# The stage behind a chunked recurrence, before and after it is cut into four quarters over all engines

## The reference, cut to what matters

```python
S_t = S_{t-1} (diag(w_t) + a_t b_t^T) + v_t k_t^T ;  y_t = S_t r_t      # y_l sums both directions

def rwkv_output(y, r, k, v, g, r_k, lnx_g, lnx_b):
    mu = jnp.mean(y, -1, keepdims=True)                  # over the 64 channels of a head
    var = jnp.mean(jnp.square(y - mu), -1, keepdims=True)
    yn = ((y - mu) * lax.rsqrt(var + GN_EPS)).reshape(B, T, D_RWKV) * lnx_g + lnx_b
    bonus = (jnp.sum(r * k * r_k, -1, keepdims=True) * v).reshape(B, T, D_RWKV)
    return (yn + bonus) * g                              # g = sigmoid(gl) @ gate_up
out_l = jnp.concatenate([att_l, rw_out_l], axis=-1) @ w_out
```

## Time and profile before

| | us |
|---|---|
| median of 3 runs | 1720.23 (1719.38 to 1720.39) |
| profiled execution, its own time | 1722.22 |
| its span, first to last instruction | 1720.4 |
| PE busy | 1532.1 (89% of the span) |
| DVE busy | 677.4 (39%) |
| ACT busy | 437.3 (25%) |
| POOL busy | 160.3 (9%) |

### The profile page before, as it was taken

One profiled execution on the slowest core, in us unless ns is written; L12 is line 12 of the kernel. 1 busy time (PEld: TensorE's weight loads), 2 busy tenths in 40 slices (PEclk: granted clock), 3 DMA queues, 4 the chain that ended last, 5 costly groups with the idle time before them and its releaser, 6 DMA issues. The chain is left out here.

```text
span 1720.4 us, 34561 instructions
## 1 busy us (share of the span) xinstructions
PE 1532.1 (89%) x15449; PEld 915.7 (53%) x15449; DVE 677.4 (39%) x1258; ACT 437.3 (25%) x947; POOL 160.3 (9%) x189
## 2 busy tenths in 40 slices
PE   5999999799999999968888886983999999999993
PEld 3445658475645555757777785443534434443431
DVE  2112025555424736744445545386131221222125
ACT  3120134352200015545454552111101101000101
POOL 3000001310001110032232330000000000000000
PEclk9999999899999998989999999995999999999997
DMA  7445530320321121000000000502699999999981
GB/s 258 147 148 213 195 111 2 79 86 13 137 73 49 49 98 47 2 2 4 3 4 4 4 4 3 222 6 92 270 427 413 409 425 406 401 426 410 403 357 73
DMA packets 48867, 278.47 MB, mean 162 GB/s; under 512 B 3784, under 2 KB 7112, under 8 KB 35920
## 3 DMA queue, kind: packets, MB, share of 16 engines
q1 hardware_dynamic: 45440, 261.96, 38.2%
q10 hardware_dynamic: 1728, 8.45, 1.2%
q0 software_dynamic: 1552, 5.85, 1.0%
HBM read 272.04 MB, written 4.19 MB: 161 GB/s over the span
## 5 line engine op out<-in xcount | busy, mean ns | idle before, releaser
L1014 PE MATMUL PS<-arena 64*64 64x64 f32 x7680 | 184.0, 222 | 34.4 <-ACT arena L1751 20.6
L1014 PEld LDWEIGHTS PS<-arena 64*64 64x64 f32 x7680 | 169.2, 134 | 52.8 <-ACT arena L1751 21.2
L1212 PE MATMUL PS<-ring,arena 128*64 128x512 f32 x288 | 128.3, 595 | 1.1 <-DVE arena L2172 1.1
L1214 PE MATMUL PS<-ring,arena 128*64 128x512 f32 x288 | 128.6, 595 | 0.0
L719 PE MATMUL PS<-arena,ring 128*128 128x512 f32 (+1 forms) x368 | 127.6, 509 | 0.0
L664 PE MATMUL PS<-ring,arena 128*128 128x512 f32 (+1 forms) x256 | 109.9, 588 | 2.5 <-ACTq L317 2.5
L757 ACT ACTIVATE arena<-PS 128x512 f32<-128x512 f32 (+3 forms) x76 | 34.8, 485 | 272.2 <-PE PS L719 112.6
L719 PEld LDWEIGHTS PS<-arena,ring 128*128 128x128 f32 x368 | 69.8, 190 | 57.7 <-issue 54.0
L1212 PE MATMUL PS<-arena 128*64 128x512 f32 x224 | 99.9, 595 | 0.0
L1214 PE MATMUL PS<-arena 128*64 128x512 f32 x224 | 99.8, 595 | 0.0
L586 DVE TENSOR_REDUCE arena<-PS 128x1 f32<-128x768 f32 (+4 forms) x96 | 62.8, 656 | 87.7 <-PE PS L494 36.0
(11 more groups left out here) (343 smaller groups left out, 2583.0 us busy)
## 6 DMA issues: line engine op xcount, KB each, us to landing
ring<-exp_w_gate SPq DMA_DIRECT2D x18, 2048.0 KB, 14.6
ring<-exp_w_up SPq DMA_DIRECT2D x18, 2048.0 KB, 10.6
ring<-exp_w_down SPq DMA_DIRECT2D x18, 2048.0 KB, 15.3
arena<-exp_w_gate SPq DMA_DIRECT2D x14, 2048.0 KB, 15.9
arena<-exp_w_up SPq DMA_DIRECT2D x14, 2048.0 KB, 12.2
arena<-exp_w_down SPq DMA_DIRECT2D x14, 2048.0 KB, 15.1
ring<-w_ada SPq DMA_DIRECT2D x12, 2048.0 KB, 12.9
ring<-w_in SPq DMA_DIRECT2D x9, 2048.0 KB, 14.8
```

Source lines behind the costliest of these rows:

```text
L1014: mm = pe.matmul(PS[i * 64:i * 64 + 64, lo:lo + 64], lhs(d, j, q), rhs(d, j, q), start=clear == "each" or clear == "bank" and (at, i) not ...
L1212: pe.matmul(bank(c, 0, 512, (0, 64)), x, unit(u)[:, k, c * 512:c * 512 + 512], start=(n == 0 and k == 0), stop=(n == 1 and k == 3))
L1214: mm = pe.matmul(bank(c, 0, 512, (64, 128)), x, unit(u + 1)[:, k, c * 512:c * 512 + 512], start=(n == 0 and k == 0), stop=(n == 1 and k == 3))
```

## The change

In the last step (g = 11) PE leaves out both products that change the state, and DVE its two instructions on S. The wait for them goes too.

The stage behind the steps is rewritten. Each group j of 512 columns runs by itself through centring (DVE), squares (ACT, `squared`), sum of squares (DVE, `variance`), root (ACT, `root_y`), reciprocal and scaling (DVE, `scaled_y`), turning (PE, `turn_y`), affine (ACT), sum with the bonus (POOL) and gate (DVE, `gated`), in an order written out by hand on each engine. The products r * r_k * k move from DVE to POOL, as two instructions for each j, and are issued right behind POOL's last mask of step 11, so beside that step. PE makes all four gates first (banks 0 to 3), without a wait, then the four bonus sums (banks 6 and 7 in turn); ACT copies each sum to SBUF (`bonus_left`), POOL multiplies it by v. `gt1_rep` (L1164) moves ahead of the last three turnings and waits for the last bonus copy, since it uses the same banks. The semaphore `pool_stage` is new. The work tiles of the last step (sg, a, P, Ee, kd, alrt0, bt, AbT, ArbT, X, XT) hold the new intermediate values.

```diff
@@ rwkv_pe, step g @@
-                product(1, 1, B, A, row_op(1), whole(W["vN"], B), clear="bank")
+                if g < 11:
+                    product(1, 1, B, A, row_op(1), whole(W["vN"], B), clear="bank")
...
-                product(1, 1, B, A, row_op(0), split(W["U"], B), clear="no").then_inc(sem("ds_done"), 1)
+                if g < 11:
+                    product(1, 1, B, A, row_op(0), split(W["U"], B), clear="no").then_inc(sem("ds_done"), 1)
...
             for j in range(4):
+                pe.matmul(bank(j), T("gateup", j * P, P), gl[:, 0:512], start=True, stop=True)
+            pe.wait_ge(sem("y_added"), 16)
+            for j in range(4):
+                pe.wait_ge(*after(f"rk{j}"))
                 if j >= 2:
-                    pe.wait_ge(sem("rw_out"), j - 1)
...
+                    pe.wait_ge(*after(f"bonus_out{j - 2}"))
+                pe.matmul(bank(6 + j % 2), C("blockones"), rk_prod(j), start=True, stop=True)\
+                    .then_inc(stage(f"bonus{j}"), 1)
+            def turn_y(j):
+                pe.wait_ge(*after(f"yn{j}"))
+                if j >= 2:
+                    pe.wait_ge(sem("yn_affine"), j - 1)
...
+            turn_y(0)
+            pe.wait_ge(*after("bonus_out3"))
...
+            for j in range(1, 4):
+                turn_y(j)
@@ DVE, step g: the two instructions on S and their waits are now under "if g < 11" @@
@@ DVE, the stage; the old block of 2048 columns and the loop over j are gone @@
+            def centred(j):
+                y, s = y_of(j), yst[:, 8 * j:8 * j + 8]
+                link(dve.tensor_reduce(s, y, AX, ALU.add))
+                link(dve.tensor_scalar(s, s, -1.0 / 64, None, ALU.mult))
+                dve.tensor_tensor(y, y, bc(s, 64), ALU.add).then_inc(stage(f"yc{j}"), 1)
+            def variance(j):
+                v = yvar[:, 8 * j:8 * j + 8]
+                dve.wait_ge(*after(f"ysq{j}"))
+                link(dve.tensor_reduce(v, y_squares(j).rearrange("p (c n) -> p c n", n=64), AX, ALU.add))
+                dve.tensor_scalar(v, v, 1.0 / 64, GN_EPS, ALU.mult, ALU.add).then_inc(stage(f"yvar{j}"), 1)
+            def scaled_y(j):
+                y, s = y_of(j), yst[:, 8 * j:8 * j + 8]
+                dve.wait_ge(*after(f"ystd{j}"))
+                link(dve.reciprocal(s, ystd[:, 8 * j:8 * j + 8]))
+                dve.tensor_tensor(y, y, bc(s, 64), ALU.mult).then_inc(stage(f"yn{j}"), 1)
+            def gated(j):
+                dve.wait_ge(*after(f"summed{j}"))
+                dve.tensor_tensor(rwT[:, j, :], rwT[:, j, :], bank(j), ALU.mult).then_inc(sem("rw_out"), 1)
+            centred(0)
+            centred(1)
+            variance(0)
+            centred(2)
+            scaled_y(0)
+            variance(1)
+            centred(3)
+            scaled_y(1)
+            variance(2)
+            scaled_y(2)
+            variance(3)
+            gated(0)
+            scaled_y(3)
+            for j in range(1, 4):
+                gated(j)
@@ ACT, the stage @@
+            def squared(j):
+                act.wait_ge(*after(f"yc{j}"))
+                act.activation(y_squares(j), T("yacc", j * 512, 512), ACT.Square).then_inc(stage(f"ysq{j}"), 1)
+            def root_y(j):
+                act.wait_ge(*after(f"yvar{j}"))
+                act.activation(ystd[:, 8 * j:8 * j + 8], yvar[:, 8 * j:8 * j + 8], ACT.Sqrt).then_inc(stage(f"ystd{j}"), 1)
+            def affine(j):
...
+            def bonus_left(j):
+                act.wait_ge(*after(f"bonus{j}"))
+                act.activation(boost(j), bank(6 + j % 2), ACT.Copy).then_inc(stage(f"bonus_out{j}"), 1)
+            bonus_left(0)
+            squared(0)
+            bonus_left(1)
+            squared(1)
+            bonus_left(2)
+            root_y(0)
+            squared(2)
+            bonus_left(3)
+            root_y(1)
+            squared(3)
+            affine(0)
+            root_y(2)
+            affine(1)
+            root_y(3)
+            affine(2)
+            affine(3)
@@ POOL, behind the 12 steps @@
+            pool.wait_ge(sem("rt_ready"), 12)
+            for j in range(4):
+                pool.tensor_scalar(rk_prod(j), rT[:, j, :], T("vec", VEC["r_k"][0] + j, 1), None, ALU.mult)\
+                    .then_inc(sem("pool_chain"), 1)
...
+                pool.tensor_tensor(rk_prod(j), rk_prod(j), kT[:, j, CTX:TOK2], ALU.mult).then_inc(stage(f"rk{j}"), 1)
+            for j in range(4):
+                pool.wait_ge(*after(f"bonus_out{j}"))
...
+                pool.tensor_tensor(b, b, vT[:, j, 4:12, :], ALU.mult).then_inc(stage(f"boosted{j}"), 1)
+            for j in range(4):
+                pool.wait_ge(sem("yn_affine"), j + 1)
+                pool.wait_ge(*after(f"boosted{j}"))
+                pool.tensor_tensor(rwT[:, j, :], rwT[:, j, :], boost(j), ALU.add).then_inc(stage(f"summed{j}"), 1)
```

More of the change, by code:

```diff
@@ L212 @@
         "hs3_std ys2_ss ys2_std hs4_std ys3_ss ys3_std hs5_std gstd_ready "
[1 row of a table removed]
[1 row of a table added]
         "o_ss o_std ").split(),
+    "pool_stage": (
+        "rk0 rk1 rk2 rk3 boosted0 boosted1 boosted2 boosted3 summed0 summed1 summed2 summed3 ").split(),
     "pe_stage": (
-        "gt1_rep gt2_rep aff_turned rank_turned ").split(),
+        "bonus0 bonus1 bonus2 bonus3 gt1_rep gt2_rep aff_turned rank_turned ").split(),
 }
@@ L953, in rk_prod, with boost, y_of, y_squares @@
         def rk_prod(j):
-            return T("scan", (4 + j) * 512, 512)
-        def kk_sq_all(n):
-            return T("scan", 0, n)
+            return W[("sg", "a", "P", "Ee")[j]]
+        def boost(j):
+            return T("scan", (SCAN.index("kd"), SCAN.index("alrt0"), SCAN.index("alrt0") + 1, SCAN.index("bt"))[j] * 512, 512)
+        def y_of(j):
+            return T("yacc", j * 512, 512).rearrange("p (c n) -> p c n", n=64)
+        def y_squares(j):
+            return W[("AbT", "ArbT", "X", "XT")[j]]
         def rwkv_pe(pe):
@@ L1149, in rwkv_pe @@
             for j in range(4):
+                pe.matmul(bank(j), T("gateup", j * P, P), gl[:, 0:512], start=True, stop=True)
+            pe.wait_ge(sem("y_added"), 16)
+            for j in range(4):
+                pe.wait_ge(*after(f"rk{j}"))
                 if j >= 2:
-                    pe.wait_ge(sem("rw_out"), j - 1)
[L1152 to L1156, removed]
+                    pe.wait_ge(*after(f"bonus_out{j - 2}"))
[5 more added lines that the diff above has]
+                    pe.wait_ge(sem("yn_affine"), j - 1)
                 for c in range(8):
                     for q in range(2):
-                        mm = pe.matmul(bank(A, c * 64, 64, (q * 64, q * 64 + 64)),
+                        mm = pe.matmul(bank(4 + j % 2, c * 64, 64, (q * 64, q * 64 + 64)),
                                        yacc[q * 64:q * 64 + 64, j, c, :], C("ident2", 0, 64, (q * 64, q * 64 + 64)),
@@ L1356, in rwkv_dve @@
                     decayed(g + 1)
[L1357 to L1362, removed]
+                if g < 11:
+                    dve.wait_ge(sem("ds_done"), g + 1)
+                    dve.tensor_tensor(both("S"), both("S"), pair(1, 1), ALU.add).then_inc(sem("s_summed"), 1)
+                    dve.wait_ge(sem("s_summed"), g + 1)
+                    dve.wait_ge(sem("wc_ready"), g + 1)
+                    st = W["S"].rearrange("p (s n) -> p s n", n=64)
+                    dve.tensor_tensor(st, st, bc(wcs[g % 2], 64), ALU.mult).then_inc(sem("s_ready"), 1)
                 if lat:
@@ L1370, in rwkv_dve @@
                             .then_inc(sem("y_added"), 1)
-            dve.wait_ge(sem("s_ready"), 12)
             dve.wait_ge(sem("y_added"), 16)
[L1373 to L1396, removed]
+            def centred(j):
[3 more added lines that the diff above has]
+                dve.tensor_tensor(y, y, bc(s, 64), ALU.add).then_inc(stage(f"yc{j}"), 1)
@@ L1756, in _ @@
                         decays_before(g + 1)
-            act.wait_ge(*after("yvar_ready"))
-            act.activation(ystd, yvar, ACT.Sqrt).then_inc(stage("ystd_ready"), 1)
-            for j in range(4):
+            def squared(j):
[5 more added lines that the diff above has]
+            def affine(j):
                 act.wait_ge(sem("rw_cols"), j + 1)
-                act.activation(rwT[:, j, :], bank(3 * (j % 2)), ACT.Identity, scale=T("vec", VEC["lnx_g"][0] + j, 1),
+                act.activation(rwT[:, j, :], bank(4 + j % 2), ACT.Identity, scale=T("vec", VEC["lnx_g"][0] + j, 1),
                                bias=T("vec", VEC["lnx_b"][0] + j, 1)).then_inc(sem("yn_affine"), 1)
+            def bonus_left(j):
[17 more added lines that the diff above has]
+            affine(3)
             phase_end(act)
```

4 lines of the change are left out of this document (3 added, 1 removed), and 2 rows, old and new, of the table STAGES.

## The result

| | before | after |
|---|---|---|
| median us (runs) | 1720.31 (4) | 1710.16 (4) |
| lowest to highest | 1719.38 to 1722.28 | 1708.82 to 1712.79 |
| ratio, 95% interval | | 0.9941 (0.9924 to 0.9959) |
| span of the profiled execution | 1720.4 | 1707.0 |

The change is 10.2 us faster (7 to 13 by the interval); 1711.7 was forecast, 1708.5 to 1716.5 the range.

A forecast was written before the change was run, and what follows sets the result against it. No engine bounded the whole; the stage behind the recurrence was a serial chain of PE, ACT and DVE. Stage with last step 6.1 us less plus next phase 2.4 made 8.5, from 1720.23 to 1711.7 us, range 1708.5 to 1716.5.

The forecast's parts named there:

- The last step: Step 11 without its state work: DVE's last addition done at 1061.91 instead of 1063.27, 1.36 us less.
- POOL beside the step: POOL's four instruction pairs in step 11 take 9.1 us, covered; holding DVE's L1337 taken as 0, at most 1.0 us.
- The stage: Pipelined stage behind the steps: ends at 1087.0 instead of 1093.09, 6.1 us less with the last step's 1.36 included.
- I take the low clock from about here: Stage, from turning 0 on: PE at low clock, turnings 1.97 us, gt1_rep 3.9; 6.1 us less, 9.1 at full clock.
- turnings of 1.97: Sign that the forecast is right: PE's turnings in the stage take 1.97 us, the low clock's length, not 1.15.
- the other end: Stage: POOL locks DVE's 8-column instructions too, giving 5.6 us less instead of 6.1, or 7.0 instead of 9.1.
- that branch: Stage at full clock with DVE's small instructions locked by POOL: 7.0 us less instead of 9.1.
- The next phase: PE enters late at low clock, covered by ln1's wait; gap shrinks to 1.3 to 3.0 us, clock kept, 2.4 less.
- Everything behind it: Routing and experts unchanged; no hidden transfer there eats the gain.
- (c): Stage: ACT reloads its table around every root, 9.0 us more; 1720.7 us, or 1724.6 with (b)'s clock and holds; chance 0.03.
- (d): Something behind the stage's fast head, such as some 30 hand-overs, gives back up to 4 us: 1715 to 1717; chance 0.1.

The follow-up runs named there:

- e1: Kernel before, with only the last step's state work left out (two PE products, two DVE instructions): 0.9996 of before, last step 8.57 us.
- e3: Kernel before, with five extra PE matmuls in the next phase's gap ahead of the turning of tile 0: 0.9983 of before.
- e6: Changed kernel with four extra PE matmuls in the next phase's gap ahead of the turning of tile 0: 0.9949 of the kernel before.
- e5: Changed kernel with ten extra PE matmuls in the stage's gaps and behind its last turning: 1712.6 us, 0.9959 of the kernel before.
- e4: Changed kernel without POOL's multiplication of the bonus by v: 0.9960 of the kernel before, stage 21.98 us.
- e8: Changed kernel without DVE's small tensor_scalar instructions in the stage, their factors taken into other instructions: 1713.2 us, 0.9962 of the kernel before.
- e2: Kernel before, with only the four products r * r_k * k moved from DVE to POOL: 1718.1 us, 0.9982 of before.

## Why the prediction was right

**The last step: right.** 1.36 us forecast, 1.54 measured, and e1 shows that it is this edit's alone. Some 0.2 of it is the spread between executions, since in e3 the unchanged step took 9.90 and not 10.11.

**POOL beside the step: right in effect.** L1337 was held no longer than before (1.04 us in both); POOL's four pairs took 12.1 us (1036.75 to 1048.81) and not 9.1, since its tensor_scalar with a scalar from SBUF takes 1.57 where the row that I took has 1.00. The first reader came at 1060.3, so this cost nothing.

**The stage: the sum nearly right, its steps in part not.** 4.7 us forecast (6.1 with the step's 1.36), 5.8 measured. The step that failed is "I take the low clock from about here", at turning 0. PE had been idle for 2.99 us there, and the turning still took 1.15. The clock fell at 1076, so turnings 0 to 2 and `gt1_rep` were fast, 2.05 instead of 3.9; of my sign "turnings of 1.97" only the last came true. The low clock also would not have cost what I gave it. In e6, whose stage is the same code, it did fall right behind turning 0 (0.50 in 1070 to 1072), and `gt1_rep` took 3.68, in e6's timeline:

```profile
1069.90 3.68 PE L1187 MATMUL PS<-arena 128*128 128x128 f32 x16
```

Yet turning 2 starts 7.1 us after turning 0 in both executions, for DVE was late enough with y to cover it, and e6's stage was 23.1 us, shorter by its last turning alone (1.15 instead of 1.97). So PE does not pace the middle of this stage, as I had it, but DVE. Where the clock falls differs between executions of the same code; on the chain it cost 0.8 us at the last turning, as e5 shows too (23.14).

What ate the rest of the gain is what I had as the other end: DVE's small instructions are held by POOL as well. Five DVE instructions that were held, four small ones and one centring, took 3.7 us more than they do alone (0.54 - 0.17, 1.70 - 0.69, 1.05 - 0.17, 1.23 - 0.17, 0.52 - 0.17). e4 and e8 took 2.0 and 2.3 us off the stage, one without POOL's work, the other without the small instructions. For that branch, the clock kept and the small ones held, my text gave 7.0 with the step; 7.4 came.

The Trainium skill, "SBUF — State Buffer", section "Who interferes with whom", has a tensor_scalar in a two-port mode among the instructions that contend with GpSimd, and the one that comes second blocks. The trace agrees as far as the small tensor_scalar goes, with 1.23 us against 0.17; in which mode it ran, no run shows.

**The next phase: the mechanism right, its size half.** 2.4 us forecast for the clock kept in the gap, and the two rows gave 0.88 + 1.60 = 2.5. 1.2 were lost at once, as `ln1` came that much later (DVE's wait 21.61 instead of 20.43), which no step of mine had. Experiments e3 and e5 move the clock in the gap, one up and one down, and the phase follows both times. PE came 2.24 us late, as forecast, but the later `ln1` widened the gap again, so it was 3.61 us and not 1.3 to 3.0. At 3.65 us the clock fell in e8. That it held here was luck in part.

**Everything behind it: right.** One table load of 1.28 us, ahead of the first root, and no wait for a load in the experts: the slower rival (c) did not occur. The number of hand-overs (d) cost nothing that shows.

Up to tile 3 the profiles gave 1.5 + 5.8 + 1.3 = 8.6, and I had forecast 8.5: terms that were off by 0.2 and 1.1 us up and by 1.1 down. That the sum is so much nearer than its terms is luck. The median's further 1.6 us (10.2 in all) are within the runs' spread of 4 us.

## What to carry to other kernels

When a serial stage is cut into a pipeline, the engines' lengths are no longer those of the serial trace: a DVE instruction that took 0.17 us takes over 1 us beside POOL. POOL's new share is better placed beside DVE's reductions (0.68 us with POOL at work, at 1063.31 after) and beside instructions that read PSUM (the gate, 0.68 at 1076.74), which kept their lengths. What follows the stage must be looked at as well: here more was to be had by issuing 1 MB ahead of 6 MB that nobody needed yet (one line, 4.6 us) than by any further work on the stage that was tried. And where PE waits in gaps like the 3.6 to 6.4 us here, the clock's fall is a term of the sum (2.5 us), as large as the edits; measure an edit there in its own stretch, not in the total.

## What the runs showed that I had not expected

- **The load of ln1 is later in every kernel with the shorter last step.** DVE's wait for it is 20.3 to 20.5 us in the three profiles without that edit (before, e2, e3) and 21.6 to 22.3 in the six with it and the old order of loads. In these six, and in none of the three, the DMA view of that stretch also shows one packet of an instruction load on a queue of its own; that of e1:

```profile
q8 instruction: 1, 0.02, 0.3%
```

  That this load of instructions delays `ln1`, and that it falls there because these kernels hold fewer instructions, are guesses from nine profiles; no run separates them.
- **Executions differ by more than some of the edits.** 2.7 us between the profiles of before and after arose at 304 to 330 us, far ahead of all that was changed: 2.2 because a DVE copy beside POOL's MEMSETs got through after one of them in eleven profiles and after two in the twelfth, where the last copy then ran into a third; and 0.5 by the clock that fell behind it. It looks like the hold of this stage once more, and who gets through first differed between executions.
- **A tensor_scalar on POOL took 1.57 us for 512 columns with its scalar in SBUF (L2399 after) and 1.00 with constants (L2291 before).**
